# Moving the exponentials of an attention unit one unit ahead on ScalarE

## What is computed

```python
def diff_attention(q, k, v, lam, lam_init, subln_g):      # 4 heads, 768 keys
    s = einsum("bhmqd,bhmkd->bhmqk", q_blk, k) * scale     # two maps m of one head
    p = softmax(s, axis=-1)
    a = p[:, :, 0] - lam * p[:, :, 1]
    o = einsum("bhqk,bhkd->bhqd", a, v)
    return rms_norm(o) * subln_g * (1.0 - lam_init)

def neighbourhood_attention(...):                          # 8 heads
    s = concatenate([s_loc + bias, s_ctx])                 # 512 local (masked) + 256 context keys
    p = softmax(s, axis=-1)
    return p @ [v_loc, v_ctx]
```

## Time and profile before

| | us |
|---|---|
| median of 3 runs (4040.48 to 4044.91) | 4044.42 |
| profiled execution, own time | 4037.23 |
| its span in the trace | 4035.4 |
| TensorE busy in the span | 3867.1 (96%) |
| ScalarE busy in the span | 1288.4 (32%) |
| granted TensorE clock, mean | 0.978 of full |

### The profile page before, as it was taken

One profiled execution on the slowest core, in us unless ns is written; L12 is line 12 of the kernel. 1 busy time (PEld: TensorE's weight loads), 2 busy tenths in 40 slices (PEclk: granted clock), 3 DMA queues, 4 the chain that ended last, 5 costly groups with the idle time before them and its releaser, 6 DMA issues.

```text
span 4035.4 us, 49523 instructions
## 1 busy us (share of the span) xinstructions
PE 3867.1 (96%) x19820; PEld 3165.9 (78%) x19820; DVE 2433.0 (60%) x4306; ACT 1288.4 (32%) x1688; POOL 470.0 (12%) x222
## 2 busy tenths in 40 slices
PE   7897788999999999999999889999999999999998
PEld 6685467888888888888888568888888888888886
DVE  3775621793799965555555240991899955555555
ACT  2224433233445542111111333333445532111111
POOL 0000023444100000000000344444000000000000
PEclk6999999999999999999999899999999999999999
DMA  6671011244454557756664130344545556656663
GB/s 229 198 233 69 22 73 53 94 143 150 166 192 181 196 204 233 261 185 200 193 191 149 42 130 6 126 141 144 185 174 205 193 195 216 196 188 199 191 194 119
DMA packets 322105, 651.25 MB, mean 161 GB/s; under 512 B 19154, under 2 KB 151891, under 8 KB 301140
## 3 DMA queue, kind: packets, MB, share of 16 engines
q1 hardware_dynamic: 285012, 580.95, 43.6%
q10 hardware_dynamic: 36864, 67.13, 4.3%
HBM read 511.69 MB, written 136.31 MB: 161 GB/s over the span
## 4 chain that ended last, share of the span: by engine, by line
PE 90%; DVE 6%; ACT 3%; issue 1%; DMA 0%; SPq 0%; DVEq 0%; ACTq 0%
PE ps L1261 35%; PE ps L1223 32%; PE ps L1141 5%; PE ps L1194 4%; PE ps L1236 4%; PE ps L1041 3%; PE ps L1067 1%; PE ps L1099 1%; PE ps L993 1%; DVE Ahot L1715 1%; PE ps L1001 1%; PE ps L1079 1%; DVE macc L1409 1%; ACT Ebuf L778 1%; PE ps L1178 1%
## 5 line engine op out<-in xcount | busy, mean ns | idle before, releaser
L1223 PE MATMUL ps<-xhi,Uhi 128*128 128x512 f32 x2048 | 811.7, 396 | 0.0
L1223 PE MATMUL ps<-xhi,Ulo 128*128 128x512 f32 x2048 | 799.6, 390 | 0.0
L1261 PE MATMUL ps<-Hlo,Vhi 128*128 128x512 f32 x2048 | 797.3, 389 | 0.0
L1261 PE MATMUL ps<-Hhi,Vhi 128*128 128x512 f32 x2048 | 797.3, 389 | 0.0
L1261 PE MATMUL ps<-Hhi,Vlo 128*128 128x512 f32 x2048 | 797.3, 389 | 0.0
L1223 PE MATMUL ps<-xlo,Uhi 128*128 128x512 f32 x2048 | 797.2, 389 | 0.0
L1742 DVE TENSOR_TENSOR Vlo<-Vraw,Vhi 128x1024 fp32r<-128x1024 f32 x256 | 313.7, 1225 | 623.6 <-ACT Vhi L927 623.5
L927 ACT CAST Vhi<-Vraw 128x1024 fp32r<-128x1024 f32 x256 | 269.5, 1053 | 1095.6 <-PE ps L1261 1076.5
L1223 PEld LDWEIGHTS ps<-xhi,Ulo 128*128 128x128 f32 x2048 | 384.6, 188 | 82.5
L1261 PEld LDWEIGHTS ps<-Hhi,Vhi 128*128 128x128 f32 x2048 | 384.6, 188 | 79.7
L1261 PEld LDWEIGHTS ps<-Hlo,Vhi 128*128 128x128 f32 x2048 | 384.6, 188 | 79.6
(11 more groups left out here) (243 smaller groups left out, 4343.1 us busy)
## 6 DMA issues: line engine op xcount, KB each, us to landing
Uraw<-in_UT SPq DMA_DIRECT2D x128, 1024.0 KB, 5.7
Vraw<-in_V SPq DMA_DIRECT2D x256, 512.0 KB, 3.7
act_scratch<-act_st ACTq DMA_DIRECT2D x256, 256.0 KB, 5.7
G_scratch<-G_st SPq DMA_DIRECT2D x32, 2048.0 KB, 8.1
act<-act_scratch SPq DMA_DIRECT2D x256, 256.0 KB, 3.5
Gin<-G_scratch SPq DMA_DIRECT2D x64, 1024.0 KB, 6.9
modw<-in_w_mod SPq DMA_DIRECT2D x80, 512.0 KB, 4.7
ring<-in_query SPq DMA_DIRECT2D x8, 2048.0 KB, 7.8
```

What stands on the lines that cost most here:

```text
L1223: mm = nc.tensor.matmul(up_bank(m), w, x[:, k, :], start=(k == 0 and j == 0), stop=(k == KT - 1 and j == 2))
L1261: mm = nc.tensor.matmul(down_bank(d), w[m % 3][:, cols], x[m % 3][:, :], start=(m == 0 and j == 0), stop=(m == NT - 1 and j == 2))
```

## The change

ScalarE's list alone is reordered. The second exponential of unit u+1 is issued in pass u, where before it was issued in pass u+1; both exponentials of unit u+1 now stand in pass u, the first behind the copy of piece 1 of unit u-1, the second behind the copy of piece 2 where there is one, and both ahead of the copy of piece 0 of unit u and of the output and square of unit u-1. Both exponentials of unit 0 come before the loop. No instruction is added or removed, and every wait is kept as it is.

```diff
             exps(0, 0)
+            exps(0, 1)
             for u in range(NU + 1):
                 if u >= 1:
                     probsT_out(u - 1, 1)
-                if u < NU:
-                    exps(u, 1)
+                if u + 1 < NU:
+                    exps(u + 1, 0)
                 if u >= 1 and maps(u - 1) == 2:
                     probsT_out(u - 1, 2)
                 if u + 1 < NU:
-                    exps(u + 1, 0)
+                    exps(u + 1, 1)
                 if u < NU:
                     probsT_out(u, 0)
                 if u >= 1:
                     outputs(u - 1)
```

## The result

The changed kernel takes 3986.88 us (median of 4 runs, 3986.36 to 3989.26) against 4042.63 (4 runs): a ratio of 0.9863, 95% interval 0.9846 to 0.9880, 56 us faster. The forecast was 3990, range 3975 to 4012. The profiled execution took 3986.36 with a span of 3984.6, 50.8 less than before.

The account below looks back on a forecast made before the run. In the attention no engine was taken as the bound, but a ring of waits; TensorE limits what follows. Gains of 24.6 (diff) and 37.1 (near) less 7.5 (clock) give 54.2, from 4044.4 to 3990 us; range 3975 to 4012.

Parts of the forecast that it names:

- the clock term: Near passes: idle times before turn(u, 0) in passes 19, 23 and 30 bring the low clock, 3 x 2.5 = 7.5 us lost.
- The ring and its link: Attention passes: engines wait on each other for the second exponential; scores stood 30.8 us in 18 waits for `Ebuf`.
- So 4.08 it is: Each diff pass: 5.79 us less TensorE's idle 1.71 before the scores gives 4.08 us.
- TensorE the bound of the diff pass, VectorE 0.23 behind: Diff pass after the change: TensorE's own list takes 4.08 us, VectorE's 3.85.
- Passes 15 and 16: Bias table of 2.29 on VectorE in pass 14: pass 15 loses 2.5 us, pass 16 another 0.2.
- Pass 19: Near pass keeping a table load of 1.28; first exponential 2.5 late, piece 2's copy waits 1.8: 7.5 us.
- Passes 23 and 27: Near passes where `nmx` follows norm and bias table; piece 2's copy comes 1.7 and 1.4 late: 7.4 and 7.1 us.
- Passes 30 to 32: Last passes; pass 30 has no scores covering piece 1's copy and four casts before it: 6.65, then 4.85 and 4.6 us.
- Sum: Whole stage: 24.6 us from diff passes plus 37.1 from near passes less 7.5 for the clock, 54.2 gained.
- Rival B: Diff passes: VectorE becomes the bound and ScalarE's slack is used up; gain 32, 4012 us; chance 0.15.
- Rival C: Attention: the two-unit ring closes in one, slower, exponentials waiting for `nmx` in every pass; 4081 us; chance 0.03.
- Rival D: End of kernel: no gain arrives, for later work waits on loads or POOL, or exponentials are held; 4044 us; chance 0.03.

## Why the prediction was right, point by point

The mechanism was right, and so was the size; that the size came out so close is partly luck, as the clock term shows.

- **The ring and its link** (waits of the scores and of `rz` for the second exponential): right. The waits of the earlier trace rows are gone, and the run with the exponential last brought them back at the price expected for it. That the release of the banks alone is enough is shown for near passes; for diff passes no run separates the two waits, and the rows say that turn(u, 0) hung on the probabilities.
- **"So 4.08 it is"**: mis-sized, 4.19. The 1.71 idle before the scores hid a wait of 0.17 that TensorE has there in every pass, where 64-row matmuls follow 128-row ones; I took the whole idle time off. And the 2.10 from the scores to turn(u, 0) was not TensorE's own list, but the time until `Abuf` was ready: it is 1.96 now, and 0.08 of the difference is lost again behind turn(u, 0). 4.08 + 0.17 - 0.14 + 0.08 = 4.19. In near passes the 0.17 stands alone: 5.85 for 5.69, and 6.32 for 6.15 with spread_roots. Together some 3 us.
- **TensorE the bound of the diff pass, VectorE 0.23 behind**: right in kind; VectorE had 0.34, since its own list took 3.85 as forecast and TensorE's was longer. (The 1.78 in that sum reaches to the start of `nmx`, not to its end, and the 0.1 to the next `rz` counts from there too; the sum stands.)
- **Passes 15 and 16**: forecast 6.6 and 4.3, measured 7.10 and 5.00. The cause, the bias table, was right and is shown by the run that moved it; I had left out that the wait in pass 15 brings the low clock (0.69 at 402 to 406). In the run with the new order in the diff passes alone the clock stayed full there, and they took 6.31 and 4.19.
- **Pass 19**: forecast 7.5, measured 8.95, and 7.32 where the clock stayed full, in the run with the square sum elsewhere (granted clock 1.00 from 422 to 434).
- **Passes 23 and 27**: forecast 7.4 and 7.1 and, in the sum, one slow stretch for 23; measured 8.93 and 8.01. VectorE's table is the cause in both, as said. It holds turn(u, 0) up by 1.5 and 0.9 (TensorE idle before it 2.44 and 1.83, in a plain pass 0.97), where 1.7 and 1.4 were forecast; the rest is the clock. **Passes 30 to 32**: forecast 6.65, 4.85 and 4.6, measured 6.50, 4.94 and 4.62.
- **The clock term, three stretches of 2.5 in passes 19, 23 and 30**: the sum was near, number, size and places were not. There were four, in passes 15, 19, 23 and 27, and none in 30, where TensorE's idle time of 2.43 is the longest of the stage. In pass 27 it fell after an idle time of 1.63, hardly longer than the 1.57 of a plain near pass before, so the length of one wait, by which I chose, does not tell. And each of the four cost about 1.6: passes 15 and 16 took 12.10 together, for 10.50 at full clock, pass 19 8.95 for 7.32, pass 23, and pass 27 with 28, as much beyond the wait. (Where the clock did fall in pass 30, in the run with the square sum elsewhere, passes 30 and 31 took 8.71 and 5.20, 2.5 more.) My 2.5 came from a pass where the clock is low in two windows (0.63 at 484 to 488, 0.52 at 488 to 492); pass 23 of the kernel after has one (0.59 at 454 to 458, 0.99 behind it). Four of 1.6 are 6.4, so the term of 7.5 was right partly by luck. The Trainium skill, "TensorE: Matmul & The Clock Gate", Part 1, as I read it, would have had all of them gone. The trace agrees by half: the stage is denser (TensorE busy 162 of 186, before 170 of 240) and the mean clock rose from 0.92 to 0.94, but four low stretches remain.
- **Sum**: 54.2 forecast, 53.6 measured in the stage. Of the 175.0 that the stage takes, the clock has 6.4 for the 7.5 forecast and the rest 168.6 for 166.9; by halves, the diff passes gained 22.1 for 24.6, the near ones 31.5 for 29.6. The misses nearly cancel. **Rival B** did not come: VectorE's operations kept their durations (1.76 for the maxima against 1.75). **Rival C** did not come: `nmx` ended at 385.62, 0.77 ahead of its exponential at 386.39, where 0.83 was forecast. **Rival D** did not come: the projection follows 4.6 behind the start of pass 32.

## What to carry to other kernels

In a ring of in-order lists, look for the instruction that two engines wait for together and ask whether its own inputs were ready long before; if so its place in the list is the cost, and one pass earlier is enough. Then size the new pass by each engine's own list, and take from an idle time only the part that has a cause you remove. The next costs are the single passes in which a seldom step stands in the list of an engine that has no slack there; moved into a wait of the same engine, it cost 0.07 at most here. Moved where there is no such wait, it costs again: the bias table in pass 1 made pass 2 take 7.10 in one of the runs.

## What the runs showed of the hardware

- Matmuls of 64 rows between matmuls of 128 cost TensorE waits of 0.17 and 0.33 us a pair, and one pair more costs 0.38 a pass. A gap inside a group of 64-row matmuls is therefore no cheap place for a 128-row one. Among 128-row matmuls the same instruction could be moved at no cost (4.19 in both places).
- The same list, with the same idle time of 2.43 us in pass 30, was followed by the low clock in one kernel (0.63 of full in the window behind it, pass 30 at 8.12) and by full clock in another (pass 30 at 6.50), while an idle time of 1.63 in pass 27 was followed by the low clock (0.57 at 482 to 486), and one of 1.57 in the kernel before was not. Pass 15 of the run with the new order in the diff passes alone took 6.31 with the same instructions that took 7.10 in the changed kernel. A single pass of a profile, where the clock is at the edge, is not a measurement of the kernel. The two rows, of the kernel before and of the changed one:

```profile
467.97 1.89 PE L1067 MATMUL ps<-kbT,qbT 64*128 64x512 f32 x8 [1.57 <-ACT Ebuf L778]
```

```profile
481.47 0.63 PE L1080 MATMUL ps<-ident,Abuf 128*128 128x128 f32 x4 [1.63 <-ACT ATbuf L787]
```

- Where an activation table is changed in the kernel before, the load takes 1.28 us and nothing is added to it: the copy before it ends at 445.45, the load starts at 445.46, and the next activation at 446.76. The Trainium skill, "ScalarE: Activation LUTs", section "What ACT_TABLE_LOAD costs", adds a drain of about the same length to every switch; this trace doesn't show one.

```profile
445.18 0.27 ACT L793 COPY oT<-ps 128x128 f32<-128x128 f32 x1 [0.89 <-PE ps L1099]
445.46 1.28 ACT L825 ACT_TABLE_LOAD   x1
446.76 0.22 ACT L825 ACTIVATE oms<-oms 128x16 f32<-128x16 f32 x1
```
